# Expert weights read in runs of 8 KB: neighbouring rows per partition, turned rows taken with a stride

## The reference, cut to what matters

```
y = (silu(x @ w_gate[e]) * (x @ w_up[e])) @ w_down[e]
```

## Time and profile before

| | us |
|---|---|
| median of three runs | 3467.81 |
| the profiled execution | 3464.86 |
| its span | 3463.3 |
| expert stage of layer 0, first turn of x rows to end of the last down product | 1838.3 to 2396.6 |
| expert stage of layer 1, the same | 2872.9 to 3433.7 |
| granted TensorE clock, mean | 0.918 of 2.4 GHz |

### The profile page before, as it was taken

One profiled execution on the slowest core, in us unless ns is written; L12 is line 12 of the kernel. 1 busy time (PEld: TensorE's weight loads), 2 busy tenths in 40 slices (PEclk: granted clock), 3 DMA queues, 4 the chain that ended last, 5 costly groups with the idle time before them and its releaser, 6 DMA issues.

```text
span 3463.3 us, 35386 instructions
## 1 busy us (share of the span) xinstructions
PE 2808.0 (81%) x12993; PEld 1760.4 (51%) x12993; DVE 1249.0 (36%) x2350; ACT 848.2 (24%) x1186; POOL 1032.6 (30%) x495
## 2 busy tenths in 40 slices
PE   4889879998998986899966777875797976787775
PEld 2668757677776765566652222221675652222221
DVE  2732233344215224742352222223437252232223
ACT  0243312234334112521121111112224221111111
POOL 0067656642874342222111000001372420000000
PEclk8999999999999998999988999998899988889998
DMA  7545478862454442032239999999251559999997
GB/s 298 180 130 186 152 260 290 289 233 77 155 167 151 145 160 82 14 111 86 97 110 329 374 371 373 376 376 335 74 158 32 199 183 333 372 375 368 377 374 265
DMA packets 366108, 780.63 MB, mean 225 GB/s; under 512 B 15076, under 2 KB 16274, under 8 KB 365216
## 3 DMA queue, kind: packets, MB, share of 16 engines
q1 hardware_dynamic: 337312, 669.61, 55.6%
q0 software_dynamic: 28672, 109.36, 9.3%
HBM read 733.58 MB, written 62.62 MB: 230 GB/s over the span
## 4 chain that ended last, share of the span: by engine, by line
PE 55%; DMA 17%; DVE 12%; issue 5%; SPq 4%; POOL 4%; ACT 3%; POOLq 0%; DVEq 0%; ACTq 0%
PE banks L720 9%; PE banks L725 9%; PE banks L721 9%; PE banks L1136 6%; PE banks L803 5%; PE banks L1114 5%; DMA arena<-moe_x 3%; DMA tokens_out<-in_moe_w_up 3%; SPq L592 3%; POOL weight_ring_r L1699 3%; DMA weight_ring<-in_moe_w_up 2%; DMA arena<-in_moe_w_down 2%; DMA weight_ring<-in_dil_w_qkv 1%; DMA rel_rows<-arena 1%; PE banks L853 1%
## 5 line engine op out<-in xcount | busy, mean ns | idle before, releaser
L1699 POOL TENSOR_TENSOR weight_ring_r<-weight_ring,weights_high_r 128x2048 fp32r<-128x2048 f32 x124 | 565.0, 4564 | 572.6 <-ACT weights_high_r L1358 443.3
L720 PE MATMUL banks<-weights_high_r,x_transposed_r 128*128 128x512 f32 x1008 | 407.1, 404 | 36.0 <-ACT weights_high_r L1358 11.5
L1358 ACT ACTIVATE weights_high_r<-weight_ring 128x2048 fp32r<-128x2048 f32 x124 | 234.4, 1898 | 768.5 <-PE banks L725 331.1
L1833 POOL DMA_DIRECT2D moe_y<-arena x64 | 33.8, 529 | 1035.2 <-DVE arena L2511 1019.0
L725 PE MATMUL banks<-weight_ring_r,x_transposed_r 128*128 128x512 f32 x1328 | 324.5, 391 | 3.0 <-POOL weight_ring_r L1699 3.0
L1699 POOL TENSOR_TENSOR weight_ring_r<-weight_ring,gates_r 128x2048 fp32r<-128x2048 f32 (+1 forms) x60 | 270.6, 4521 | 140.8 <-ACT gates_r L1358 79.7
L725 PEld LDWEIGHTS banks<-weight_ring_r,x_transposed_r 128*128 128x128 f32 x1328 | 248.7, 188 | 58.0 <-POOL weight_ring_r L1699 6.6
L1114 PE MATMUL banks<-weight_ring,arena 128*64 128x512 f32 x1024 | 240.9, 604 | 41.9 <-DMA weight_ring<-in_moe_w_up 25.5
L720 PEld LDWEIGHTS banks<-weights_high_r,x_transposed_r 128*128 128x128 f32 x1008 | 193.7, 192 | 93.8 <-issue 29.6
L1564 ACT ACTIVATE arena<-banks 64x1024 f32<-64x1024 f32 x64 | 65.3, 1020 | 595.6 <-PE banks L1114 595.6
L2493 DVE TENSOR_TENSOR arena<-banks,arena 64x1024 f32<-64x1024 f32 x64 | 77.8, 1216 | 352.1 <-ACT arena L1564 352.1
(11 more groups left out here) (368 smaller groups left out, 4673.9 us busy)
## 6 DMA issues: line engine op xcount, KB each, us to landing
weight_ring<-in_moe_w_gate SPq DMA_DIRECT2D x64, 1024.0 KB, 15.7
weight_ring<-in_moe_w_up SPq DMA_DIRECT2D x64, 1024.0 KB, 15.1
weights_high<-in_moe_w_down SPq DMA_DIRECT2D x64, 1024.0 KB, 16.1
x_transposed<-in_moe_w_gate SPq DMA_DIRECT2D x60, 1024.0 KB, 16.2
tokens_out<-in_moe_w_up SPq DMA_DIRECT2D x60, 1024.0 KB, 15.6
arena<-in_moe_w_down SPq DMA_DIRECT2D x60, 1024.0 KB, 16.2
weight_ring<-in_w_in SPq DMA_DIRECT2D x56, 1024.0 KB, 5.2
weight_ring<-in_w_ada SPq DMA_DIRECT2D x48, 1024.0 KB, 7.2
```

The source lines that it names most:

```text
L720: nc.tensor.matmul(banks[t][:, 0:width], xh, wh[:, k, :], start=k0 + k == 0, stop=False)
L1358: nc.scalar.activation(high(s, kn, width), slot(c, kn, width), ACT.Copy).then_inc(high_ready, 1)
L1699: nc.gpsimd.tensor_tensor(slot(c, kn, width, ring_r), slot(c, kn, width), high(s, kn, width), ALU.subtract).then_inc(low_ready, 1)
```

## The change

A partition now takes four neighbouring rows of gate or up for each half (row p * 8 + g * 4 + k), 8 KB that lie together in DRAM. A half of down is two neighbouring rows in full width (row p * 4 + g * 2 + k), 8 KB too; so a half of down is no longer half of the columns but half of the contraction. To match, the transposition k of the x rows takes every eighth column from k on, and that of the hidden rows every fourth. The down product has the same eight products; each half now serves both banks, with two parts of the contraction. The overflow loops are changed in the same way; they are left out below.

```diff
             def load_gate_up / load_down
-                        src = I[name][layer].rearrange("e (g k p) n -> e g p k n", p=P, k=KG)
+                        src = I[name][layer].rearrange("e (p g k) n -> e g p k n", p=P, k=KG)
...
-                    src = I["moe_w_down_2"][layer].rearrange("e (k p) (g n) -> e g p k n", p=P, g=2)
-                    sp.dma_start(slot(c, KG, BANK), src[e, half]).then_inc(w_in[slots[c]], 16)
+                    src = I["moe_w_down_2"][layer].rearrange("e (p g k) n -> e g p k n", p=P, k=2)
+                    sp.dma_start(slot(c, 2, D), src[e, half]).then_inc(w_in[slots[c]], 16)
...
-                    last = waiting_turn(ps[4][:, 0:CAP], A[0:CAP, E_X + par * D:E_X + par * D + P])
+                    last = waiting_turn(ps[4][:, 0:CAP], A[0:CAP, E_X + par * D:E_X + (par + 1) * D:KD])
                     for k in range(1, KD):
                         last = nc.tensor.transpose(ps[4][:, k * CAP:(k + 1) * CAP],
-                                                   A[0:CAP, E_X + par * D + k * P:E_X + par * D + (k + 1) * P],
+                                                   A[0:CAP, E_X + par * D + k:E_X + (par + 1) * D:KD],
                                                    ident[0:CAP, 0:CAP])
...
-                    last = waiting_turn(ps[5][:, 0:CAP], A[0:CAP, E_HD + par * 512:E_HD + par * 512 + P])
+                    last = waiting_turn(ps[5][:, 0:CAP], A[0:CAP, E_HD + par * 512:E_HD + (par + 1) * 512:4])
                     for k in range(1, 4):
                         last = nc.tensor.transpose(ps[5][:, k * CAP:(k + 1) * CAP],
-                                                   A[0:CAP, E_HD + par * 512 + k * P:E_HD + par * 512 + (k + 1) * P],
+                                                   A[0:CAP, E_HD + par * 512 + k:E_HD + (par + 1) * 512:4],
                                                    ident[0:CAP, 0:CAP])
...
                     for half in range(2):
-                        w = slot(next_chunk(i, per_turn), KG, BANK)
-                        for k in range(4):
-                            h = A[:, E_HT + par * 256 + k * CAP:E_HT + par * 256 + (k + 1) * CAP]
-                            last = nc.tensor.matmul(halves(ps[2 + half], k), h, w[:, k, :], start=k < 2, stop=k >= 2)
+                        w = slot(next_chunk(i, per_turn), 2, D)
+                        for n in range(2):
+                            for k in range(2 * half, 2 * half + 2):
+                                h = A[:, E_HT + par * 256 + k * CAP:E_HT + par * 256 + (k + 1) * CAP]
+                                last = nc.tensor.matmul(halves(ps[2 + n], k), h, w[:, k % 2, n * BANK:(n + 1) * BANK],
+                                                        start=half == 0, stop=half == 1)
                         last.then_inc(d_ready if half == 1 else w_used, 1)
```

More of the change, by code:

```diff
@@ L238, in over_down @@
         def over_down(half):
-            return spare[:, half * KG * BANK:(half + 1) * KG * BANK].rearrange("p (k n) -> p k n", k=KG)
+            return spare[:, half * KG * BANK:(half + 1) * KG * BANK].rearrange("p (k n) -> p k n", k=2)
         w_in = [sem(f"weights_arrived_{i}") for i in range(E_RING)]
@@ L1169, in experts @@
                         pe.wait_ge(over["x_in"], counted(pe, 16 * j + 16))
-                        last = waiting_turn(ps[4][:, 0:CAP], A[0:CAP, E_X:E_X + P])
+                        last = waiting_turn(ps[4][:, 0:CAP], A[0:CAP, E_X:E_X + D:KD])
                         for k in range(1, KD):
                             last = nc.tensor.transpose(ps[4][:, k * CAP:(k + 1) * CAP],
-                                                       A[0:CAP, E_X + k * P:E_X + (k + 1) * P], ident[0:CAP, 0:CAP])
+                                                       A[0:CAP, E_X + k:E_X + D:KD], ident[0:CAP, 0:CAP])
                         last.then_inc(over["xT"], 1)
@@ L1183, in experts @@
                         pe.wait_ge(over["hidden"], counted(pe, j + 1))
-                        last = waiting_turn(ps[5][:, 0:CAP], A[0:CAP, E_HD:E_HD + P])
+                        last = waiting_turn(ps[5][:, 0:CAP], A[0:CAP, E_HD:E_HD + 512:4])
                         for k in range(1, 4):
                             last = nc.tensor.transpose(ps[5][:, k * CAP:(k + 1) * CAP],
-                                                       A[0:CAP, E_HD + k * P:E_HD + (k + 1) * P], ident[0:CAP, 0:CAP])
+                                                       A[0:CAP, E_HD + k:E_HD + 512:4], ident[0:CAP, 0:CAP])
                         last.then_inc(over["hiddenT"], 1)
@@ L1191, in experts @@
                             w = over_down(half)
[L1192 to L1195, removed]
+                            for k in range(2 * half, 2 * half + 2):
+                                for n in range(2):
+                                    last = nc.tensor.matmul(halves(ps[2 + n], k),
+                                                            A[:, E_HT + k * CAP:E_HT + (k + 1) * CAP],
+                                                            w[:, k % 2, n * BANK:(n + 1) * BANK],
+                                                            start=half == 0, stop=half == 1)
                         last.then_inc(over["down"], 1)
```

## The result

The changed kernel takes 3624.09 us (median of 4 runs, 3621.68 to 3627.09); the kernel before took 3468.18 us in the same comparison. The ratio is 1.0462, 95% interval 1.0447 to 1.0478: slower by 156 us where 18 were forecast, and outside the range of 3415 to 3535.

A forecast was written before the change was run, and what follows sets the result against it. Bounded by a 17.0 us loop per expert, hidden at first, then weight supply at 18.1. Per layer 7 x 18.8 + 21 x 17.9 = 507.5: +16.9 and +14.0, less 12.6, gives +18.3, 3486 us at the median; range 3415 to 3535.

The forecast's parts named there:

- The two bounds: In the expert stages: a loop of 17.0 us per expert, hidden at first, and a supply of weights at 18.1.
- part (1): Weight packets of 8 KB: supply falls from 18.1 to 16.6 us per expert, while the x fetch lands 1.8 us later.
- its signs: Expected in the new profile, among others: some 100,000 packets on the SP queue, turned loads staying at 140 ns.
- The forecast case: Later x rows lengthen the loop to 18.8 us for 7 experts, 17.9 for 21: 3486 us, chance 0.45.
- Eight weight packets ... 8 x 0.223 = 1.8 us.: On each DMA engine eight weight packets pass between those of store and fetch, each 223 ns longer, delaying the fetch 1.8 us.
- 0.9 back, an estimate: After 7 experts SP's shorter backlog leaves 1.8 us of work before a store instead of 2.7, so 0.9 us returns.
- Strided turns: I take 0.: Turning x and hidden rows on TensorE with strided loads adds nothing to the loop; upper bound 1.5 us per expert.
- Down split: 0.: Splitting the down product over the contraction costs 0: same 8 products and loads, both banks written before the same signal.
- Tail: 12.6 us won.: Weight waits after a layer's last turn, 6.3 us in layer 0, disappear; taken twice, 12.6 us.
- the fetch stays in time: Rival: the shorter backlog takes back what longer packets add, the loop stays 17.0 us; 3423 us, chance 0.33.
- No gain in rate: Rival: weight packets stay 2 KB or 8 KB ones move no more bytes per second; 3468 us, chance 0.10.
- turned loads cost: Rival: strided loads in TensorE's turns add 1.5 us per expert to the loop; 3507 to 3570 us, chance 0.12.

The follow-up runs named there:

- experiment 5: Each fetch of x rows issued one expert earlier: on the kernel before 3463.47 us (ratio 1.0003), on the changed kernel 3392.08 us (0.9799).
- experiment 3: The changed kernel with all weights in runs of 4 KB instead of 8 KB: 3538.70 us, ratio 1.0212 to the kernel before.
- experiment 1: Contiguous turns on the changed kernel: 3620.02 us, ratio 1.045; strided turns alone on the kernel before: 3467.03 us, ratio 1.0016.

## Why the prediction was wrong

**The two bounds** of loop and supply were right: give the fetch one expert more and the steps follow the weights in both kernels (experiment 5). The supply came to 17.0 us with 8 KB packets, where 16.6 were forecast, and weights alone pass at 426 GB/s (2.98 MB in 7 us of that kernel), where 420 were. **The direction and the mechanism** of part (1) were right too: packets of 8 KB, the one-to-one turn between the queues, a fetch that pays for all of it, waits for weights gone, DMA share below 1. One of its signs was wrong besides the number of packets: turned loads did not stay at 140 ns. Weight packets took 310 ns against 308. The forecast case held; its size did not. The forecast had 507.5 us for 28 steps, and 571.9 and 574.8 came: 132 us too few in 56 steps. By its terms:

- *"Eight weight packets ... 8 x 0.223 = 1.8 us."* It measured 2.7. Four packets beside the store cost 4 x 0.224 = 0.9 us, as forecast, but four beside the fetch cost 4 x 0.309 = 1.24, since each takes 424 ns there, not 308; the rest is 0.2 us at the start and about one packet more on each engine (68 weight packets beside the store and 82 beside the fetch, where four each make 64). The forecast named this as its upper bound (3 us) and did not take it. 0.9 x 56 = 50 us.
- *"0.9 back, an estimate"* from a shorter backlog. This step failed outright. The backlog did shrink (landing 15.7 to 9.5 us), yet the store's first packet still came 4.14 us after its issue. The step expected 1.8 us of work in the queues when the store reaches them, some 0.7 MB; 1.9 MB were outstanding, and 1.65 of them went ahead (experiment 3). With early fetches weights land after 30 us, and the packet comes at 3.71. So a backlog of 1.9 MB and one of 9.5 cost a store the same, and by the stores at the ends of the stages only one below some 1.6 MB gives anything back, down to 1.1 us with none. 0.9 x 42 = 38 us.
- *"Strided turns: I take 0."* It measured 0.62 of a bound of 1.5. A load of the same shape was the nearest row, and the trace showed no stride; but it did show turns at the lower level, as the longest loads of the earlier trace rows hint. Seven of 54 ran at 0.50 and took 1.36. Either gives the price here, and experiment 1 shows that the clock would have taken it without the stride: the longer idle time forecast in part (1) had a cost of its own at its end, which the sum left out. 0.62 x 56 = 35 us. The Trainium skill (SBUF — State Buffer, Door 1: The DMA port swizzle) lets accesses that go to a new 16-byte line each time lose bandwidth; by that rule the trace agrees at a step of 32 bytes, 202 ns against 141. At a step of 8 bytes, with two values on each such line, it does not: the loads of the 4 KB variant with early fetches take 220, at a granted clock of 1.00.
- *Down split: 0.* Right within 0.1: 5.45 us in the mean against 5.33, and part of that may be the clock. The variant that kept the split and the 8 KB runs of down lost 0.9% in all.
- *Tail: 12.6 us won.* Right: from the last turn to the end of the last down product 24.3 and 24.2 us pass, where 30.8 and 30.5 did, 12.8 less together. What follows on the stages took 2.5 us more, so that 4.4 + 5.9 = 10.3 are left behind the last turns. The start of the stages, +9.7, was not in the sum: the loop binds there too.

Two lines belong to the third point: one of the seven turns on the kernel before, at 0.50 behind a wait for weights, and the loads of the 4 KB variant with early fetches:

```profile
2222.33:2223.70 1.37, 1.37 (x12) 1.25 (x10) 0.20 (x1) 1.02 (x1) 0.00 (x0) 0.50 1.07 392
```

```profile
L1094 PEld LDWEIGHTS banks<-constants,arena x448: 210/220/334, 1827.1 to 3350.1; 64*128 64x128 f32 x150
```

50 + 38 + 35 is 123 of the 132; the down product holds 7 of the other 9 (0.12 x 56). With the starts, the 2.3 us that the ends are short of 12.6 and the 2.5 ahead of the first stage, 132 + 9.7 + 2.3 - 2.5 is 141, and 18.3 + 141 = 159 us, the difference of the spans.

The rival *the fetch stays in time* failed with the 0.9. *No gain in rate* is false: 398 GB/s against 373 once nothing else binds. By the rule of 512 B in the Trainium skill (DMA: Bandwidth & Descriptors, Specifications) there would be nothing to gain; by these rows the trace does not agree. Of *turned loads cost* the cause is there in the loads, at less than half its bound, and invisible in the time as the kernel stands.

What is open: why some 1.6 MB of weights pass ahead of a store's first packet, and not all that are outstanding. Nothing was run that changes GpSimd's queue itself. What makes a weight packet slower beside a fetch is likewise only measured (115 and 424 ns), not explained.

## What to carry to other kernels

Before making the transfers of one queue longer, look for a small transfer on another queue that something waits for: it takes its turn one packet for one, so its delay grows with the others' packets. Give it slack first (here each fetch is issued for one expert further ahead), then lengthen the runs: alone the first is worth nothing and the second costs 4.6%, together they win 2.0% (1.9 in the repetition). And where an idle stretch of TensorE grows, price what runs right after it at the lower clock as well.

## What was not expected of the hardware

- A strided load of fp32 columns takes 202 ns against 141 in TensorE at a step of 8 values, and 220 at a step of 2. It is hidden where the granted clock is 0.50: there contiguous ones take 221.
- After 3.7 us of idle TensorE the turn still ran at a granted clock of 1.00 (0.80 us), after 5.7 at 0.50 (1.36 us). In both kernels the down product behind it has a part at the lower level (0.68 and 0.67 in the mean of its stretch).
- Weight packets beside a fetch into 64 partitions are slower than beside a store from them: 424 and 310 ns at 8 KB, 219 and 159 at 4 KB, 115 and 86 at 2 KB.
- The time from the issue of a store to its first packet is 3.7 to 4.2 us with 1.9 MB of weights outstanding or 9.5, and 1.1 us with none.
